# First pair of each MLP summed and split ahead of it, tile chains in another order, mean square in a bank of its own

## What is computed

```python
h = h + s5_mixer(rmsnorm(h, norm_mix[0]), ...)            # ends in val * sigmoid(gate), the GLU
h = h + sq_relu_mlp(rmsnorm(h, norm_mlp[0]), w_in[0], w_out[0])
k, v = split(rmsnorm(h, norm_kv) @ w_kv + b_kv)
h = h + attention(rmsnorm(h, norm_mix[1]), k, v, ...)     # window 128, learned sinks, ends in @ w_o
h = h + sq_relu_mlp(rmsnorm(h, norm_mlp[1]), w_in[1], w_out[1])
out = rmsnorm(h, norm_final)

def rmsnorm(x, g): return x * rsqrt(mean(x * x) + 1e-5) * g
def sq_relu_mlp(h, w_in, w_out): return square(relu(h @ w_in)) @ w_out    # 1024 -> 4096 -> 1024
```

## Time and profile before

| | us |
|---|---|
| median of three runs | 1065.13 |
| the profiled execution | 1064.35 |
| its span, first to last instruction | 1062.6 |
| TensorE busy | 1016.1 (96%) |
| VectorE busy | 757.3 (71%) |
| ScalarE busy | 464.0 (44%) |
| GpSimd busy | 306.9 (29%) |

### The profile page before, as it was taken

One profiled execution on the slowest core, in us unless ns is written; L12 is line 12 of the kernel. 1 busy time (PEld: TensorE's weight loads), 2 busy tenths in 40 slices (PEclk: granted clock), 3 DMA queues, 4 the chain that ended last, 5 costly groups with the idle time before them and its releaser, 6 DMA issues.

```text
span 1062.6 us, 18055 instructions
## 1 busy us (share of the span) xinstructions
PE 1016.1 (96%) x6634; PEld 868.7 (82%) x6634; DVE 757.3 (71%) x1063; ACT 464.0 (44%) x872; POOL 306.9 (29%) x256
## 2 busy tenths in 40 slices
PE   9799999899999999989999999979999999999896
PEld 4677888789999899888777666857899899899886
DVE  8993368986787777774845764788777777878535
ACT  7862123544444344433314885344444444444321
POOL 8996866300000000012947220950000000002040
PEclk9899999999999999999999999988999999999998
DMA  6123333223222312320322110422322322233012
GB/s 246 37 46 122 119 117 121 80 99 120 99 79 93 144 62 96 118 80 21 100 85 100 61 40 1 142 76 99 120 77 83 132 85 99 96 122 118 21 40 80
DMA packets 31881, 97.58 MB, mean 92 GB/s; under 512 B 10696, under 2 KB 13256, under 8 KB 27984
## 3 DMA queue, kind: packets, MB, share of 16 engines
q1 hardware_dynamic: 31824, 96.83, 26.5%
HBM read 92.36 MB, written 2.10 MB: 89 GB/s over the span
## 4 chain that ended last, share of the span: by engine, by line
PE 75%; DVE 13%; issue 6%; ACT 4%; POOL 1%; POOLq 0%; DMA 0%; DVEq 0%; ACTq 0%
PE ps L1634 9%; PE ps L1636 9%; PE ps L1635 9%; PE ps L1654 8%; PE ps L1655 8%; PE ps L1656 8%; PE ps L1594 5%; PE ps L1596 4%; PE ps L1595 4%; ACT act L666 1%; PE ps L1820 1%; PE ps L1540 1%; PE ps L1795 1%; PE ps L1542 1%; PE ps L1541 1%
## 5 line engine op out<-in xcount | busy, mean ns | idle before, releaser
L439 POOL TENSOR_TENSOR gate_sb<-gate_sb 128x1 f32<-128x1 f32 x60 | 21.7, 361 | 720.9 <-DMA raw<-panels_in 519.8
L1654 PE MATMUL ps<-hid,w_hi 128*128 128x512 f32 x384 | 151.8, 395 | 6.1 <-DVE hid L1125 6.1
L1655 PE MATMUL ps<-hid,w_hi 128*128 128x512 f32 x384 | 151.5, 395 | 0.0
L1656 PE MATMUL ps<-hid,w_lo 128*128 128x512 f32 x384 | 150.3, 391 | 0.0
L528 POOL TENSOR_TENSOR w_lo<-raw,w_hi 128x1024 fp32r<-128x1024 f32 x60 | 148.7, 2479 | 5.0
L1634 PE MATMUL ps<-hid,s_hi 128*128 128x256 f32 x448 | 127.3, 284 | 5.5 <-issue 5.4
L1635 PE MATMUL ps<-hid,s_hi 128*128 128x256 f32 x448 | 127.3, 284 | 0.0
L1636 PE MATMUL ps<-hid,s_lo 128*128 128x256 f32 x448 | 127.3, 284 | 0.0
L1104 DVE TENSOR_TENSOR s_lo<-w_raw,s_hi 128x1024 fp32r<-128x1024 f32 (+1 forms) x112 | 109.7, 991 | 19.4 <-ACT s_hi L691 18.7
L1594 PE MATMUL ps<-hid,w_hi 128*128 128x512 f32 x304 | 120.7, 397 | 0.0
L1595 PE MATMUL ps<-hid,w_hi 128*128 128x512 f32 x304 | 118.8, 391 | 0.0
(11 more groups left out here) (267 smaller groups left out, 2201.6 us busy)
## 6 DMA issues: line engine op xcount, KB each, us to landing
raw<-panels_in SPq DMA_DIRECT2D x108, 512.0 KB, 3.3
w_raw<-pairs_in SPq DMA_DIRECT2D x28, 1024.0 KB, 5.4
xy<-xu_in SPq DMA_DIRECT2D x4, 512.0 KB, 7.4
out<-h SPq DMA_DIRECT2D x8, 256.0 KB, 2.2
prm<-prm_in SPq DMA_DIRECT2D x1, 1280.0 KB, 5.6
h<-x_rows_in SPq DMA_DIRECT2D x1, 1280.0 KB, 12.8
h<-x_rows_in SPq DMA_DIRECT2D x1, 768.0 KB, 7.7
dd<-dd_in SPq DMA_DIRECT2D x1, 256.0 KB, 5.8
```

The source lines that it names most:

```text
L1654: mm(to, w_hi[:, s, w], hid[:, 0, 0, HK * par + k, :], start=(k == 0), stop=False)
L1655: mm(to, w_hi[:, s, w], hid[:, 0, 1, HK * par + k, :], start=False, stop=False)
L1656: last = mm(to, w_lo[:, s, w], hid[:, 0, 0, HK * par + k, :], start=False, stop=(k == HK - 1))
```

## The change

- SBUF is laid out anew: `s_lo`, `s_hi`, then `w_raw`, so that `w_raw` no longer shares bytes with attention's tiles. `load_pair(0)` is issued after panel 7 in GLU, `load_pair(PAIRS)` after the fourth query panel; the second pair of each MLP is loaded after its fourth panel, once all seven blocks of the first are split.
- The first pair of the first MLP is summed and split on VectorE after GLU tiles 1 to 4 (`head_sums`, `head_rest`, `head_last_sum`) and on ScalarE after tiles 1 and 3 (`head_round`); that of the second MLP in steps 16 to 18 of attention's `skewed`. The fourth sum goes to a block of `w_raw` in place of `t1`.
- `first_relu` writes to `first_raw`, which lies where `first_low` writes its result, in place of two slots of `t2`. All four relus stand ahead of all four lows.
- After the first MLP, a tile's add is followed by the q low half and the square sum of the tile before, then by its own kv low half. After attention, the square sum of the tile before stands between the add and the low half, and the T blocks are made after tiles 5, 6 and (two) 7, in place of one after each of tiles 4 to 7.
- The mean square of the MLPs' norms is in bank 4, in place of 7, so `stats` no longer waits for the T blocks. TensorE waits for T blocks and for the whole first pair ahead of the first step.
- In the last two steps `last_near(0)` stands in the first gap, `last_near(1)` and `last_near(2)` are cut in halves over two gaps, `last_near(3)` follows the last product.

```diff
--- before.py
+++ after.py
@@ -78,6 +78,8 @@
 FIRST, FOURTH, SECOND, THIRD, LAST = (A11, A12), (S1, A22), (S2,), (S3,), (S4,)
+HEAD = (FIRST, SECOND, THIRD, FOURTH, LAST)
+HEAD_S4 = 2
@@ -172,7 +174,7 @@
         sq_sum = ps[:, 4, :]
-        stat = ps[:, 7, :]
+        stats_of = (ps[:, 4, :], ps[:, 7, :], ps[:, 4, :])
@@ -220,12 +222,16 @@
+        plain = ExitStack()
+        sb("below", [P, KT, L], where=plain)
+        first_raw = sb("first_raw", [P, HK, L], where=plain)
+        plain.close()
 ...
         act = sb("act", [P, 2, KT, L], F32R, where=over)
+        s_lo = sb("s_lo", [P, 7, HK * P], F32R, where=over)
+        s_hi = sb("s_hi", [P, 7, HK * P], F32R, where=over)
         w_raw = sb("w_raw", [P, 6, HK * P], where=over)
-        s_hi = sb("s_hi", [P, 7, HK * P], F32R, where=over)
-        s_lo = sb("s_lo", [P, 7, HK * P], F32R, where=over)
@@ -341,9 +347,9 @@
-        def raw_blocks(blocks):
+        def raw_blocks(blocks, head=False):
             if blocks == LAST:
-                return t1[:]
+                return w_raw[:, HEAD_S4, :] if head else t1[:]
@@ -395,31 +401,32 @@
-                wait(sp, s_split, 7 * n - 3)
+                wait(sp, s_split, 7 * n - (0 if n % PAIRS == 1 else 3))
 ...
                 base, n0 = U_MLP[layer], PAIRS * layer
-                load(base, base + 1)
-                load_pair(n0)
-                load(base + 1, base + 7)
+                load(base, base + 4)
                 load_pair(n0 + 1)
-                load(base + 7, base + 8)
+                load(base + 4, base + 8)
 ...
-            load(4, U_MLP[0])
+            load(4, 8)
 ...
             wait(sp, unit_done, U_GLU + 2)
+            load_pair(0)
+            load(8, U_MLP[0])
 ...
             sp.dma_start(mask[:], mask_d).then_inc(s_mask, 16)
-            load(U_Q, U_MLP[1])
-            wait(sp, ot_lo, QUADS * NBLK)
+            load(U_Q, U_Q + 4)
+            load_pair(PAIRS)
+            load(U_Q + 4, U_MLP[1])
@@ -691,10 +698,20 @@
+            def head_round(n, blocks):
+                a.wait_ge(pair_in, 16 * n + 16)
+                wait(a, prod_done, 7 * n)
+                first, last = blocks[0], blocks[-1]
+                if first in SUM_OF:
+                    a.wait_ge(s_sum, 3 * n + SUM_OF[first])
+                act_fn(s_hi[:, first:last + 1, :].rearrange("p b n -> p (b n)"), raw_blocks(blocks, head=True), ACT.Copy
+                       ).then_inc(s_hi_done, 1)
 ...
                 wait(a, stat_v, 2 * n + 2)
-                act_fn(rstd[:], stat, ACT.Sqrt).then_inc(stat_a, 1)
+                act_fn(rstd[:], stats_of[n], ACT.Sqrt).then_inc(stat_a, 1)
@@ -708,19 +725,20 @@
                     t_his(0, m - HK, "g_mlp0")
+                for blocks in {1: HEAD[:4], 3: (LAST,)}.get(m, ()):
+                    head_round(0, blocks)
 ...
                 base = U_MLP[layer]
-                for blocks in (FIRST, FOURTH, SECOND, THIRD, LAST):
-                    s_round(n0, blocks, 7 * n0 or None)
 ...
                 for m in range(HK):
+                    low = first_raw[:, m, :]
                     a.wait_ge(hid_sq, HK * layer + m + 1)
-                    act_fn(t2[:, m % 2, :], t2[:, m % 2, :], ACT.Square).then_inc(first_sq, 1)
+                    act_fn(low, low, ACT.Square).then_inc(first_sq, 1)
                     a.wait_ge(first_sq, HK * layer + m + 1)
-                    act_fn(hid[:, 0, 0, m, :], t2[:, m % 2, :], ACT.Copy).then_inc(hid_hi, 1)
+                    act_fn(hid[:, 0, 0, m, :], low, ACT.Copy).then_inc(hid_hi, 1)
@@ -829,13 +847,17 @@
-            skewed([(norm_p, 1), (o_hi, 3), (turned, 2), (exps, 0)])
+            def next_pair(Q):
+                for blocks in {QUADS * NBLK: HEAD[:1], QUADS * NBLK + 1: HEAD[1:4], QUADS * NBLK + 2: HEAD[4:]}.get(Q, ()):
+                    head_round(PAIRS, blocks)
+            skewed([(norm_p, 1), (o_hi, 3), (turned, 2), (exps, 0), (next_pair, None)])
 ...
                 norm_hi(2, m, [("g_mlp1", act)])
-                if m >= HK:
-                    t_his(1, m - HK, "g_mlp1")
+                for k in {5: (0,), 6: (1,), 7: (2, 3)}.get(m, ()):
+                    t_his(1, k, "g_mlp1")
@@ -1029,12 +1051,23 @@
                 if m > 0:
-                    v.wait_ge(sq_tmp, norm * KT + m + 1)
-                    wait(v, sq_acc, norm * (KT - 1) + m - 1)
-                    tt(acc[:] if m == KT - 1 else sq_sum, sq_sum, t2[:, m % 2, :], ALU.add).then_inc(sq_acc, 1)
+                    square_sum(norm, m)
+            def square_sum(norm, m):
+                v.wait_ge(sq_tmp, norm * KT + m + 1)
+                wait(v, sq_acc, norm * (KT - 1) + m - 1)
+                tt(acc[:] if m == KT - 1 else sq_sum, sq_sum, t2[:, m % 2, :], ALU.add).then_inc(sq_acc, 1)
+            def low_half(n, g, dst, m):
+                v.wait_ge(n_hi, n)
+                stt(dst[:, 1, m, :], h[:, m, :], COLS(g)[:, m:m + 1], dst[:, 0, m, :].bitcast(F32),
+                    ALU.mult, ALU.subtract).then_inc(n_lo, 1)
 ...
+                stat = stats_of[n]
@@ -1065,6 +1098,29 @@
+            def head_sums(n):
+                v.wait_ge(pair_in, 16 * n + 16)
+                wait(v, s_split, 7 * n)
+                tt(w_raw[:, 0:4:3, :], w_raw[:, 1:5:3, :], w_raw[:, 3, :].unsqueeze(1).to_broadcast([P, 2, HK * P]), add
+                   ).then_inc(s_sum, 1)
+                v.wait_ge(s_sum, 3 * n + 1)
+                tt(raw_blocks(SECOND), w_raw[:, RAW_OF[S1], :], w_raw[:, RAW_OF[A11], :], add).then_inc(s_sum, 1)
+            def head_last_sum(n):
+                v.wait_ge(s_sum, 3 * n + 2)
+                v.wait_ge(s_split, 7 * n + 2)
+                tt(raw_blocks(LAST, head=True), raw_blocks(SECOND), w_raw[:, RAW_OF[A12], :], add).then_inc(s_sum, 1)
+            def head_rest(n, blocks):
+                first, last = blocks[0], blocks[-1]
+                v.wait_ge(s_hi_done, 5 * n + HEAD.index(blocks) + 1)
+                tt(s_lo[:, first:last + 1, :].rearrange("p b n -> p (b n)"), raw_blocks(blocks, head=True),
+                   s_hi[:, first:last + 1, :].rearrange("p b n -> p (b n)").bitcast(F32), sub
+                   ).then_inc(s_split, len(blocks))
@@ -1079,6 +1135,17 @@
                     t_blocks(0, m - HK, "g_mlp0")
+                if m == 1:
+                    head_sums(0)
+                elif m == 2:
+                    head_rest(0, FIRST)
+                    head_last_sum(0)
+                    head_rest(0, SECOND)
+                    head_rest(0, THIRD)
+                elif m == 3:
+                    head_rest(0, FOURTH)
+                elif m == 4:
+                    head_rest(0, LAST)
@@ -1114,32 +1181,22 @@
                     v.wait_ge(unit_done, base + m + 1)
-                    if m > 1:
-                        v.wait_ge(hid_lo, FB * HK * layer + m - 1)
-                    stt(t2[:, m % 2, :], ps[:, (m + shift) % 4, :], 0.0, rstd[:], ALU.max, ALU.mult).then_inc(bank_free, 1)
+                    stt(first_raw[:, m, :], ps[:, (m + shift) % 4, :], 0.0, rstd[:], ALU.max, ALU.mult
+                        ).then_inc(bank_free, 1)
 ...
                     v.wait_ge(hid_hi, FB * HK * layer + m + 1)
-                    tt(hid[:, 0, 1, m, :], t2[:, m % 2, :], hid[:, 0, 0, m, :].bitcast(F32), ALU.subtract).then_inc(hid_lo, 1)
-                sums(p0)
-                rest(p0, FIRST)
+                    tt(hid[:, 0, 1, m, :], first_raw[:, m, :], hid[:, 0, 0, m, :].bitcast(F32), ALU.subtract
+                       ).then_inc(hid_lo, 1)
                 inverse(norm)
-                rest(p0, FOURTH)
                 wait(v, stat_a, STAT_A[norm])
-                first_relu(0)
-                first_relu(1)
-                rest(p0, SECOND)
-                first_low(0)
-                first_low(1)
-                rest(p0, THIRD)
-                rest(p0, LAST)
-                first_relu(2)
-                first_relu(3)
-                first_low(2)
-                first_low(3)
+                for m in range(HK):
+                    first_relu(m)
+                for m in range(HK):
+                    first_low(m)
@@ -1265,11 +1322,18 @@
                         v.wait_ge(bank_free, 4 + V0 + 1 + m)
-                        if layer == 0:
-                            normed(1, KT + 2 * m, m, [("g_kv", act), ("g_q", hid[:, 1])])
+                        v.sem_inc(h_added, 1)
+                        if layer:
+                            normed(3, 4 * KT, m, [])
                         else:
-                            normed(3, 4 * KT, m, [])
-                        v.sem_inc(h_added, 1)
+                            if m > 0:
+                                low_half(KT + 2 * m, "g_q", hid[:, 1], m - 1)
+                            if m > 1:
+                                square_sum(1, m - 1)
+                            low_half(KT + 2 * m + 1, "g_kv", act, m)
+                    if layer == 0:
+                        square_sum(1, KT - 1)
```

(40 more changed lines are left out.)

## The result

The changed kernel takes 1038.6 us, the median of four runs (1035.0 to 1042.3), against 1065.9 for the kernel before in the same session: a ratio of 0.974, 95% interval 0.971 to 0.978. The predicted time was 1037.0.

What follows compares the result with a forecast made beforehand. TensorE, busy 96% of the span, bounds the kernel, so gains come only from its pauses and lower-clock stretches. 4.3 + 7.1 + 4.3 + 11.6 = 27.3 us off 1064.35 gives 1037.0 us, range 1031.0 to 1044.0.

Steps and rivals of the forecast that it cites:

- Start of the first MLP: First MLP's start: earlier rstd and lows let product S2 start at 209.8 instead of 214.06; gain 4.3 us.
- the cover in GLU and at attention's end: GLU and attention's end: the first pairs' moved sums and splits fit idle gaps; cost nothing, 0 to 1 us as bound.
- End of each MLP: Last steps of both MLPs: near matmuls fill TensorE's pauses; 2.7 us each, plus 1.7 of clock at the second.
- K/V: K/V projection: last tile comes earlier and statistics run at full clock; gain 4.3 us, bounds 1.5 to 5.9.
- the walk through the first cycle: K/V projection: two low halves fit GpSimd's first cycle, so the last kv half comes at 531.0 instead of 533.8.
- The clock term: K/V projection: the 1.5 us pause left is too little for the lower clock; 1.5 if only the statistics run faster.
- Start of the second MLP: Second MLP's start: fewer T blocks ahead of tile 7, S2 at 724.6 instead of 737.40; gain 11.6 us, bounds 9 to 15.4.
- the tie: Second MLP, tile 6: low half and `w_lo` arrive within 0.1 us; forecast gave GpSimd the port, leaving a 2.7 us pause.
- rival (a): Second MLP, tile 6: VectorE gets the port first, hardly a pause, 2.2 + 1.7 us better, 1033.1; chance 0.25.
- (b): Both tile chains: GpSimd's lock sets every tile, so they gain nothing; 1046 us, chance 0.17.
- (c): First MLP and GLU: lows miss the first output tile or the pair's transfer holds queues; 1 to 4 us, 1040, chance 0.10.
- (d): Product matmuls: new SBUF places cost each more than 12 ns, making the kernel slower; 1072 at 15 ns, chance 0.03.

Runs made afterwards that it cites:

- holds_head_late: Changed kernel with both GpSimd waits, first pair of the first MLP summed and split behind the last T block again: 1043.7 us, 11.1 above the kernel with both waits.
- kv_old: Changed kernel with the old order of square sum and low halves after the first MLP: 1043.8 us, 4.6 to 5.1 above the changed kernel.
- after_again: The changed kernel unaltered, run and profiled a second time: median 1039.2 us, its profiled run 1041.3 us.
- near_only: Kernel before with only the near halves of the last output units moved between the last products: 1060.4 us, 3.5 below the kernel before.
- after: First profile of the changed kernel, unaltered: the profiled execution took 1035.0 us.
- chain_old: Changed kernel with the old order after attention, square sum behind the low half and a T block after each of tiles 4 to 7: 1044.5 us.
- bank7: Changed kernel with the mean square of the MLPs' norms in bank 7 again, waiting for the T blocks: 1044.9 us, 5.8 to 6.3 above.
- two holds: Changed kernel with GpSimd waiting for VectorE's low halves before the third K/V panel and the second MLP's fourth panel: 1033.9 and 1032.6 us.

## Why the prediction was right, and where not

- **Start of the first MLP**: 4.3 predicted, 4.5 in the trace; every time told for after (rstd, relu 3, lows, S2) came within 0.3 us, and the cover in GLU and at attention's end cost nothing. Which part made the gain, the pair's new place or the new order of relus and lows, no run separates cleanly; holds_head_late speaks for the order.
- **End of each MLP**: 2.7 each predicted; the first gave 2.8, the second 4.3 with its clock, as forecast (4.4). Two experiments give 3.5 and 7.6 us for both ends, by what happens to the clock elsewhere.
- **K/V**: 4.3 predicted, 2.9 in the trace: 1.4 from an earlier last tile, where 2.8 was predicted, and 1.5 from the clock, as predicted. The step that failed is the walk through the first cycle: it had the q half of tile 0 and the kv half of tile 1 both pass before `w_lo`. The q half passed, the kv half came 0.37 us too late. What gain there was in the chain came from what the walk held constant, GpSimd's cycle: 4.41 us in place of 4.62, since `w_hi` now takes 1.05 us where kv_old shows 1.57, while `w_lo` takes 2.71 where it shows 2.41. Seven such cycles are 1.5 us, kv_old's 1.3. So the pause left is 2.8 us, not 1.5; in after_again 6.83 us of lower clock follow it and the seam gains nothing. The clock term came from one profile (3.41 us); kv_old and near_only have 10.24 us behind the same pause. That it came out at 1.5 is in part luck.
- **Start of the second MLP**: 11.6 predicted, 14.9 in the trace. The walk was right up to the tie, and the size of its stake nearly (2.2 us and 1.7 of clock told, 2.05 and 1.1 between after and after_again): the profiled run took rival (a). In after_again the forecast's branch came true, pause 2.9 us against 2.7 told, one stretch of 3.41 us behind it, and the seam gives 11.7 us. chain_old and bank7 show that the new tile order and the new bank were both needed: without the first the kernel takes 5.3 to 5.8 us more, without the second 5.8 to 6.3.
- **Rivals**: (b) fell by its numbers, since chain_old and kv_old are slower, but its mechanism holds in K/V: GpSimd's cycle sets every tile there, and only a shorter cycle gained. (c) fell, the pair's transfer held nobody. (d) fell: the products keep their pace of 0.12 us in the new place.

So the total was near because four of the five terms were right by their steps, for the branch that most profiles take; the 1035.0 of the profiled run was the rarer one. With the seams as after gives them, but the second MLP's start as after_again does, the sum is 4.5 + 2.8 + 2.9 + 11.7 + 4.3 = 26.2 us, or 1038.2, an estimate beside the median of 1038.6. Luck is in it as well: the lower clock moves a run by up to 3 us at one seam (after and after_again). In the traces the tie and the clock behind two pauses carry the 6.3 us between after and after_again; two holds that remove these pauses or shorten them leave a spread of 3.9 us in place of 7.5, and some 5 us less time. Which of the other runs took which branch has no trace.

## What to carry to other kernels

Where two engines share a lock, a chain can hang on a tie of some 0.03 us: look for it, take a second profile before trusting one, and let the engine off the critical path wait explicitly through the other's chain. A tile order pays only with the queue behind it free: ask of each moved step which matmul, transfer or `w_lo` stands behind the thing it waits for. And price a TensorE pause like these (2.7 to 4.7 us) as the pause and the half-clock stretch that may follow, from more than one profile.

## What was not expected of the hardware

- The record's start doesn't tell who gets the lock: VectorE's low half starts 0.02 to 0.03 us before `w_lo` and is held (687.12 and 687.14, 685.43 and 685.46), 0.05 us before it and goes through (684.02 and 684.07). The Trainium skill (SBUF — State Buffer, section "Who interferes with whom") says that whoever issues first gets the shared ports for the whole instruction; the traces agree in the second half of that (VectorE's held operation takes 2.97 us in place of 0.74, GpSimd's 2.96 in place of 2.40), and leave the first open below 0.05 us.
- The same pause of 2.8 us ahead of the last K/V tile was followed by no stretch at the lower clock in the profile after and by 6.83 us of it (0.50, 1.2 GHz) in after_again, one kernel at one place. TensorE ran without a pause over 0.5 us for hundreds of us before it in both. The pause of 3.75 us of the old order was followed by 3.41 us in the kernel before and by 10.24 in near_only and kv_old.
